# Two attentions and a recurrence ahead of the feed-forward layers: transposes, projections and norms taken in another order

## The chip, the cores and the metric

The kernel runs on one core of a Trainium2 chip. The metric is the device time of one execution in microseconds: 1994.58 as the median of three runs (1994.4 to 1996.17). Engines are TensorE (PE: products and transposes), VectorE (DVE), ScalarE (ACT), GpSimd (POOL) and SyncE (SP, which issues nearly all transfers).

## The reference

Two transformer layers are computed for 256 positions of width 1024. The change touches the first one, up to its feed-forward part. In the reference it reads, cut to that part:

```
h = rms_norm(x, attn_norm); proj = h @ w_in
lru_out = (hf + hb) * gelu(yg)            # two gated recurrences over the 256 positions, forward and back
q = rms_norm((c_q @ w_uq) per head, q_norm);  k = rms_norm(concat(k_nope, k_rope), k_norm)   # 8 heads of 96
q, k: the last 32 of 96 columns rotated (rope)
mla_out = softmax(q k^T * 96 ** -0.5) v
mixed = concat(rms_norm(lru_out), rms_norm(mla_out));  x = x + mixed @ w_out
q = rms_norm((rms_norm(x) @ w_mem_q) per head);  k = rms_norm((mem_n @ w_mem_kv) per head)   # 4 heads of 128
x = x + (softmax(q k^T * 128 ** -0.5) v) @ w_mem_o
x = x + (silu(g) * u) @ w_down            # feed-forward, not changed
```

A row norm divides a row by one number. So `rms_norm(mla_out) @ w` can be taken as `mla_out @ w` whose rows are then divided, and a query's norm can be a factor on its row of scores. A rotation does not change the sum of squares that the norm needs.

## The kernel before, in words

Weights arrive as units of 128 x 2048 numbers (1 MB) in seven buffers `raw`. ScalarE rounds a unit to the high part `wh` (`hi_to(n)` makes all units below n), VectorE subtracts it to get the low part `wl` (`lo_to(n)`); there are three pairs (`SPLIT`), so the high part of unit n waits until TensorE has released unit n-3, and the load of unit n waits for the low part of unit n-7. A product is taken in three passes (`split_product`): high by high, low by high, and, after a wait for `wl`, high by low. Activations have their own high and low parts, `hTh` and `hTl`. Units 0 to 5 are `w_in`, 6 to 9 `w_mem_kv`, 10 `w_uq`, 11 `w_ukv`, 12 to 15 `w_out`, 16 and 17 `w_mem_q`, 18 and 19 `w_mem_o`, from 20 on the feed-forward weights.

Each engine runs a list written out by hand; engines meet at semaphores (`reached(name, count)`). Nothing is planned or reordered. The order of the stages on TensorE: norm of x and `w_in`; gates of the recurrence; memory keys and values; `w_uq`, the ones-product that sums the squares of the recurrence (`lru_ssq`), `w_ukv`; transposes of query and key heads (`mla_qkT_ps`, line 536, 16 and 16); `attention("mla")`, eight heads in a pipeline of scores, transposed probabilities and weighted values, with eight pieces of the first half of `w_out` (`mixed`, n = 0 and 1) between them; transposes of the attention's output (`mla_oT_ps`); the second half of `w_out` (n = 2 and 3); x transposed; `w_mem_q`; transposes; `attention("mem")`, four heads; transposes; `w_mem_o`.

On VectorE, between the recurrence and the attention, stand `head_ms` (reduction of squares per head), the scaling of the recurrence's output (`lru_std`, `lru_scaled`), and `rotated`, which multiplies a whole of 16 heads x 96 by its inverse root and then rotates: the query first, then the key. In `attention`, VectorE takes the largest score (line 1959), ScalarE the exponentials (1322) and the copy of transposed probabilities (1330), VectorE the division by the sum (1968). ScalarE functions come in table sets: a root after an exponential shows an `ACT_TABLE_LOAD`.

The softplus series for `lru_lambda` (`sp`, 8 columns, 17 tiny operations, each waiting for the last) runs on VectorE just ahead of `lo_to(8)`.

## Time and profile before

| what | us |
|---|---|
| median of 3 runs | 1994.58 |
| profiled execution: own time / span | 1991.48 / 1989.6 |
| TensorE busy | 1883.1 (95%) |
| VectorE, ScalarE busy | 1555.6 (78%), 1253.9 (63%) |
| last chain of work, share on PE / DVE / ACT | 87% / 7% / 4% |
| first matmul on a weight unit starts | 15.33 |
| first transposes of query heads start | 111.11 |
| first scores start | 119.60 |
| memory queries' projection starts | 174.76 |
| last product of `w_mem_o` ends | 224.22 |

The part that the change touches ends at 224.22 us; the other 1765 us are the feed-forward part and the second layer. A timeline row gives start, length, engine, line, operation, output<-inputs, shapes and count, and in brackets the idle time before it with the engine that ended it. Busy time of a matmul row includes its pipeline, so the cost of one in a row of them is the distance between starts. The granted clock (PEclk) is a share of 2.4 GHz.

### The profile page before, as it was taken

What the parts mean: (1) busy time and instruction counts of PE and PEld (TensorE: products, weight loads), DVE (VectorE), ACT (ScalarE), POOL (GpSimd) and SP (SyncE); (2) the same over time, 40 slices, a digit from 0 to 9 for tenths busy, and PEclk for the clock granted to TensorE, in tenths of its full rate; (3) what the DMA queues carried; (4) which work ended last, traced back from release to release, by engine and by line L of the source; (5) the groups of instructions that cost most, each with busy time, mean ns of one, the idle gap of its engine ahead of it and who ended that gap; (6) DMA issues with size and microseconds to landing.
All of it is one profiled execution on the core that took longest, in us unless ns stands there. A gap on an engine that the chain in (4) does not pass through costs nothing.

```text
span 1989.6 us, 27408 instructions
## 1 busy us (share of the span) xinstructions
PE 1883.1 (95%) x10192; PEld 1586.2 (80%) x10192; DVE 1555.6 (78%) x1572; ACT 1253.9 (63%) x1285; POOL 11.3 (1%) x9
## 2 busy tenths in 40 slices
PE   7867899999899999998799999999999999999997
PEld 7755799887789988876688888888888888888886
DVE  7865588657656755665798998989989889899897
ACT  6854565455644435553577777777777777777775
POOL 0000000000000000000100000000000000000000
PEclk9988999999889999999899999999999999999998
DMA  8322244543225554433399998998989989999894
GB/s 356 127 101 85 85 180 181 191 171 125 85 106 189 175 188 152 149 124 105 144 370 345 339 372 322 365 364 330 367 323 361 371 326 363 330 363 367 318 367 187
DMA packets 68040, 490.83 MB, mean 247 GB/s; under 512 B 7680, under 2 KB 7936, under 8 KB 8576
## 3 DMA queue, kind: packets, MB, share of 16 engines
q1 hardware_dynamic: 67680, 488.52, 65.7%
q0 software_dynamic: 288, 1.31, 0.2%
q8 instruction: 50, 0.82, 0.2%
q14 instruction: 22, 0.18, 0.0%
HBM read 488.75 MB, written 1.05 MB: 246 GB/s over the span
## 4 chain that ended last, share of the span: by engine, by line
PE 87%; DVE 7%; ACT 4%; issue 2%; DMA 0%; SPq 0%; ACTq 0%; DVEq 0%
PE ps L399 26%; PE ps L401 20%; PE ps L408 20%; PE ps L410 5%; PE ps L403 5%; PE ps L419 2%; DVE wl L1887 1%; PE ps L1182 1%; ACT wh L1258 1%; PE ps L1094 1%; PE ps L913 1%; DVE hTl L1927 1%; PE ps L950 1%; PE ps L953 0%; PE ps L686 0%
## 5 line engine op out<-in xcount | busy, mean ns | idle before, releaser
L2713 DVE TENSOR_TENSOR wl<-raw,wh 128x2048 fp32r<-128x2048 f32 x336 | 763.1, 2289 | 81.4 <-ACT wh L1811 81.3
L1811 ACT ACTIVATE wh<-raw 128x2048 fp32r<-128x2048 f32 x336 | 642.6, 1917 | 196.3 <-PE ps L408 196.0
L399 PE MATMUL ps<-wh,work_r 128*128 128x512 f32 x1544 | 614.7, 398 | 4.0 <-DVE work_r L2718 2.4
L401 PE MATMUL ps<-wh,work_r 128*128 128x512 f32 x1544 | 613.4, 397 | 0.0
L408 PE MATMUL ps<-wl,work_r 128*128 128x512 f32 x1544 | 449.6, 396 | 0.0
L1887 DVE TENSOR_TENSOR wl<-raw,wh 128x2048 fp32r<-128x2048 f32 x125 | 286.1, 2290 | 128.0 <-ACT wh L1258 127.5
L399 PEld LDWEIGHTS ps<-wh,work_r 128*128 128x128 f32 x1544 | 290.6, 188 | 71.4 <-issue 6.9
L408 PEld LDWEIGHTS ps<-wl,work_r 128*128 128x128 f32 x1544 | 290.4, 188 | 70.2
L401 PEld LDWEIGHTS ps<-wh,work_r 128*128 128x128 f32 x1544 | 290.6, 188 | 68.9
L1258 ACT ACTIVATE wh<-raw 128x2048 fp32r<-128x2048 f32 x125 | 238.6, 1913 | 156.2 <-PE ps L408 88.9
L399 PE MATMUL ps<-hTh,wh 128*128 128x256 f32 x896 | 223.8, 287 | 2.0 <-DVE hTl L1927 1.8
L403 PE MATMUL ps<-hTl,wh 128*128 128x256 f32 x896 | 221.8, 285 | 0.0
L399 PEld LDWEIGHTS ps<-hTh,wh 128*128 128x128 f32 x896 | 173.5, 194 | 4.3 <-issue 2.6
L403 PEld LDWEIGHTS ps<-hTl,wh 128*128 128x128 f32 x896 | 173.5, 194 | 0.1
L410 PE MATMUL ps<-hTh,wl 128*128 128x256 f32 x896 | 126.3, 284 | 0.0
L410 PEld LDWEIGHTS ps<-hTh,wl 128*128 128x128 f32 x896 | 116.2, 193 | 0.0
L399 PE MATMUL ps<-wh,hTh 128*128 128x512 f32 (+1 forms) x216 | 89.3, 414 | 6.4 <-DVE hTl L2181 1.8
L401 PE MATMUL ps<-wh,hTl 128*128 128x512 f32 (+1 forms) x216 | 85.6, 397 | 0.0
L1821 ACT ACTIVATE work<-ps 128x512 f32<-128x512 f32 x56 | 33.6, 600 | 46.0 <-PE ps L408 45.9
L408 PE MATMUL ps<-wl,hTh 128*128 128x512 f32 (+1 forms) x216 | 62.6, 396 | 0.0
L419 PE MATMUL ps<-work 128*128 128x64 f32 (+2 forms) x240 | 43.5, 323 | 14.5 <-DVE xn L2293 3.4
L1496 ACT ACTIVATE xn<-ps,cols 128x256 f32<-128x256 f32 x44 | 22.4, 560 | 52.2 <-PE ps L410 52.2
(391 smaller groups left out, 1715.0 us busy)
## 6 DMA issues: line engine op xcount, KB each, us to landing
raw<-in_units SPq DMA_DIRECT2D x461, 1024.0 KB, 6.7
x<-in_x SPq DMA_DIRECT2D x1, 1024.0 KB, 4.9
work<-in_lru_w SPq DMA_DIRECT2D x1, 1024.0 KB, 15.2
xn<-in_mem SPq DMA_DIRECT2D x1, 1024.0 KB, 16.5
out<-x SPq DMA_DIRECT2D x2, 512.0 KB, 3.3
consts<-in_consts POOLq DMA_DIRECT2D x1, 768.0 KB, 4.7
work<-in_moe_gain POOLq DMA_DIRECT2D x1, 512.0 KB, 3.8
consts<-in_consts SPq DMA_DIRECT2D x1, 488.0 KB, 5.7
```

What stands on the lines that cost most here:

```text
L399: nc.tensor.matmul(out, sh, mh, start=(first and j == 0), stop=False)
L401: nc.tensor.matmul(out, sl, mh, start=False, stop=False)
L403: nc.tensor.matmul(out, sh, ml, start=False, stop=False)
L408: ins = nc.tensor.matmul(out, sh, ml, start=False, stop=done)
L410: ins = nc.tensor.matmul(out, sl, mh, start=False, stop=done)
L419: ins = nc.tensor.matmul(out, l, r, start=(first and j == 0), stop=(last and j == len(pairs) - 1))
L1258: A(wh[:, n % SPLIT, :], raw[:, n % RAW, :], ACT.Copy).then_inc(sem("hi_made"), 1)
L1496: ins = A(cv[f % 4][i], ps[:, f % 4, i * S:(i + 1) * S], ACT.Identity, scale=col("ffn_conv_w", 2 * FT + c), bias=col("ffn_conv_b", c))
L1811: A(wh[:, n % SPLIT, :], raw[:, n % RAW, :], ACT.Copy).then_inc(sem("hi_made"), 1)
L1821: A(esg, ps[:, 2 * (c % 2), :], ACT.Sigmoid).then_inc(sem("sigmoid"), 1)
L1887: V.tensor_tensor(wl[:, n % SPLIT, :], raw[:, n % RAW, :], wh[:, n % SPLIT, :].bitcast(F32), ALU.subtract).then_inc(sem("lo_made"), 1)
L2713: V.tensor_tensor(wl[:, n % SPLIT, :], raw[:, n % RAW, :], wh[:, n % SPLIT, :].bitcast(F32), ALU.subtract).then_inc(sem("lo_made"), 1)
```

## The change

- Start: `cols` is transferred first, x in two halves on two semaphores, of the constants only the first 272 of 976 columns ahead of the weights, the other 704 behind unit 2. The softplus series is taken at the very start, while x arrives, and its exponential stands ahead of the first norm.
- Recurrence to attention: the low part of unit 11 is made ahead of the backward recurrence; `w_ukv` goes ahead of the ones-product. The query is rotated without having been multiplied; its inverse root goes as a scale into the exponential (and, by one more small operation for each head, into the largest score). The key's 32 rotary columns are rotated once, before they are copied to the heads, and their squares are summed once. Buffers move so that this can overlap. VectorE's subtraction for the recurrence's output (`lru_outT`) moves behind the first largest score.
- First attention: the pieces of `w_out` start one head later. n = 0 and 1 are closed as a sum of their own and added to x during the attention (`lru_added`); the first two output chunks are transposed within head iteration 8; n = 2 and 3 are not divided by the root beforehand, but at the sum: x += r * (their product).
- Memory attention: `w_mem_q` in two units by columns (two heads each), so that two heads can be normed while the other two are projected; key transposes go ahead of the projection; the order of all steps on the three engines is written out; `w_mem_o`'s first half stands between the last two heads. The query's inverse roots are scales of the exponentials here too.

The core of the diff:

```diff
-        sp_.dma_start(x[:], x_d).then_inc(sem("x_loaded"), 16)
-        small_consts = CONST["dist"]
-        sp_.dma_start(cols[:], cols_d).then_inc(sem("params"), 16)
-        sp_.dma_start(consts[:, 0:small_consts], consts_d[:, 0:small_consts]).then_inc(sem("params"), 16)
+        sp_.dma_start(cols[:], cols_d).then_inc(sem("cols_loaded"), 16)
+        for t in range(TT):
+            sp_.dma_start(x[:, t, :], x_d[:, t, :]).then_inc(sem(f"x{t}_loaded"), 16)
+        early = CONST["reset"]
+        sp_.dma_start(consts[:, 0:early], consts_d[:, 0:early]).then_inc(sem("params"), 16)
...
+            if n == 2:
+                sp_.dma_start(consts[:, early:CONST["dist"]], consts_d[:, early:CONST["dist"]]).then_inc(sem("consts_loaded"), 16)
...
# TensorE
-        attention("mla", [lambda n=n, t=t, h=h: mixed(n, t, h, False) for n in range(2) for t in range(TT) for h in range(2)])
-        pe.wait_ge(*reached("mla_normed", TT))
-        transposes("mla_oT_ps", [mo[:, t, c * P:(c + 1) * P] for c in range(LC) for t in range(TT)], [0, 1], "")
+        def first_mixed():
+            pe.wait_ge(*reached("lru_outT", 1))
+            mixed(0, 0, 0)
+        def last_of_recurrence():
+            mixed_oT(0)
+            mixed(1, 1, 1)
+        def first_of_attention():
+            pe.wait_ge(*reached("mla_oT", 2))
+            mixed(2, 0, 0)
+        attention("mla", [lambda: None, first_mixed]
+                  + [lambda i=i: mixed(i // 4, i // 2 % 2, i % 2) for i in range(1, 7)]
+                  + [last_of_recurrence, first_of_attention])
+        mixed(2, 0, 1)
+        mixed_oT(1)
+        mixed(2, 1, 0)
+        mixed(2, 1, 1)
...
-        token_major("mem_in", UNITS_AT["w_mem_q"], hTh, hTl, (4, 5))
-        attention("mem")
-        transposes("mem_oT_ps", [eo[:, t, c * P:(c + 1) * P] for c in range(4) for t in range(TT)], [0, 1], "")
-        project_out("memory_x_change", UNITS_AT["w_mem_o"], 4, hTh, hTl, lambda k: None)
+        pe.wait_ge(*reached("mem_heads_normed", 1))
+        for u in range(2):
+            mem_turned(6 + u, [ek[:, t, h * P:(h + 1) * P] for h in (2 * u, 2 * u + 1) for t in range(TT)])
+        mem_query(0, 0)
+        mem_query(0, 1)
+        mem_query(1, 0)
+        pe.wait_ge(*reached("mem_in_copied", 5))
+        mem_turned(2, [eq[:, t, h * P:(h + 1) * P] for h in (0, 1) for t in range(TT)])
+        mem_query(1, 1)
+        mem_score(0)
+        mem_score(1)
+        pe.wait_ge(*reached("mem_in_copied", 6))
+        mem_turned(3, [eq[:, t, h * P:(h + 1) * P] for h in (2, 3) for t in range(TT)])
+        mem_turn(0)
+        mem_score(2)
+        mem_weigh(0)
+        mem_turn(1)
+        mem_score(3)
+        mem_weigh(1)
+        mem_turn(2)
+        mem_oT(0)
+        mem_weigh(2)
+        mem_turn(3)
+        mem_out(0, 0)
+        mem_out(0, 1)
+        mem_weigh(3)
+        mem_out(0, 2)
+        mem_oT(1)
+        mem_out(0, 3)
+        for q in range(4):
+            mem_out(1, q)
...
# VectorE
+        def lru_added(q):
+            dve.wait_ge(*reached("mixer_x_change", q + 2))
+            xs = x[:, q // 2, (q % 2) * HALF:(q % 2 + 1) * HALF]
+            V.tensor_tensor(xs, ps[:, 4 + q, :], xs, ALU.add).then_inc(sem("lru_added"), 1)
-        attention("mla", {1: lambda: lo_to(14), 3: lambda: lo_to(15), 4: mem_key_squares, 6: lambda: lo_to(16)})
+        attention("mla", {0: lru_low, 2: lambda: lo_to(14), 3: mem_key_squares, 4: lambda: lo_to(15),
+                          6: lambda: lru_added(0), 7: lambda: (lru_added(1), lo_to(16)),
+                          8: lambda: (lru_added(2), mla_oT_low(0), lru_added(3))})
+        mla_oT_low(1)
...
+                V.scalar_tensor_tensor(out=xs, in0=ps[:, 4 + 2 * t + h, :], scalar=osq["r"][:, t:t + 1], in1=xs,
+                                       op0=ALU.mult, op1=ALU.add).then_inc(sem("x_ready"), 1)
```

First place, VectorE from the gate product of the recurrence (`gelu`) to the first rotated heads. `wl<-raw,wh` is the low part of a weight unit, `mla_squares` the squares of the heads. Before:

```order
L2117 TENSOR_TENSOR work<-work 128x1024 [waits gelu,vector_step]
L1887 TENSOR_TENSOR wl<-raw,wh 128x2048 [waits hi_made]
L2147 TENSOR_SCALAR work<-ps 128x256 [waits lru_ssq]
L2123 TENSOR_REDUCE heads_st<-work 128x16 [waits mla_squares]
L2124 TENSOR_SCALAR heads_st<-heads_st 128x16 [waits vector_step]
L2150 RECIPROCAL work<-work 128x256 [waits std]
L2152 SCALAR_TENSOR_TENSOR work<-work,cols 128x256 [waits vector_step]
L2152 SCALAR_TENSOR_TENSOR work<-work,cols 128x256 x3
L1887 TENSOR_TENSOR wl<-raw,wh 128x2048 [waits hi_made]
L2123 TENSOR_REDUCE heads_st<-work 128x16 [waits mla_squares]
L2124 TENSOR_SCALAR heads_st<-heads_st 128x16 [waits vector_step]
L2130 RECIPROCAL heads_st<-heads_st 128x16 [waits std]
```

After (`hT_f_49`, `hT_f_50` are plain views of `hTh`, `hTl`, in which the squares and the key now lie):

```order
L2328 TENSOR_TENSOR work<-work 128x1024 [waits gelu,vector_step]
L2332 TENSOR_REDUCE heads_st<-hT_f_49 128x16 [waits mla_squares]
L2333 TENSOR_SCALAR heads_st<-heads_st 128x16 [waits vector_step]
L2340 TENSOR_TENSOR hT_f_49<-work,junk 128x256
L2341 TENSOR_TENSOR hT_f_49<-work,junk 128x256
L2342 TENSOR_TENSOR hT_f_49<-work,junk 128x256
L2343 TENSOR_TENSOR hT_f_49<-work,junk 128x256
L2344 TENSOR_TENSOR work<-hT_f_49 128x16x16 [waits vector_step]
L2345 TENSOR_TENSOR work<-hT_f_49 128x16x16
L2083 TENSOR_TENSOR wl<-raw,wh 128x2048 [waits hi_made]
L2349 TENSOR_SCALAR work<-ps 128x256 [waits lru_ssq]
```

The six query rotations stood behind two reductions, a reciprocal of 256 columns, four scalings, a weight unit and a product over 1536 columns; now they follow the first reduction. The low part of unit 11, which stood behind the gate product, stands ahead of the piece shown.

Second place, ScalarE in the memory attention, from the copy of a query projection to the third head's exponentials. `wh<-raw` is a weight unit's high part, `[waits in]` a projection, `[waits ms]` a root. Before:

```order
L1476 ACTIVATE work<-ps,small 128x512 [waits in]
L1310 ACTIVATE heads_st<-heads_st 128x8 [waits ms]
L1481 ACTIVATE work<-ps,cols 128x256 [waits qkT_ps] x8
L1322 ACT_TABLE_LOAD
L1322 ACTIVATE work,small<-ps,small 128x256 [waits att_max]
L1322 ACTIVATE work,small<-ps,small 128x256
L1322 ACTIVATE work,small<-ps,small 128x256 [waits att_max]
L1322 ACTIVATE work,small<-ps,small 128x256
L1330 ACTIVATE work<-ps 128x512 [waits att_transposed]
L1322 ACTIVATE work,small<-ps,small 128x256 [waits att_max]
```

After:

```order
L1397 ACTIVATE wh<-raw 128x2048 [waits in,raw_loaded5]
L1631 ACTIVATE work<-ps 128x2x256 [waits in]
L1645 ACTIVATE work,small<-ps,small,heads_st 128x256 [waits att_max]
L1645 ACTIVATE work,small<-ps,small,heads_st 128x256
L1625 ACTIVATE work<-ps,cols 128x512 [waits qkT_ps]
L1653 ACTIVATE work<-ps 128x512 [waits att_transposed]
L1645 ACTIVATE work,small<-ps,small,heads_st 128x256 [waits att_max]
L1645 ACTIVATE work,small<-ps,small,heads_st 128x256
L1637 ACT_TABLE_LOAD
L1637 ACTIVATE heads_st<-heads_st 128x4 [waits ms]
L1653 ACTIVATE work<-ps 128x512 [waits att_transposed]
L1645 ACT_TABLE_LOAD
```

Copies, roots, turned queries and exponentials, which followed each other as blocks, now alternate, and a root stands between the second and the third pair of exponentials, with a table load on each side.

## Rows read from the trace of the kernel before

**Rows 1.** Windows: three stretches; busy us and instructions per engine, clock, DMA, GB/s.

```profile
0.00:119.60 119.60, 86.38 (x483) 77.60 (x483) 97.67 (x173) 88.13 (x142) 0.92 (x5) 0.93 0.56 217
119.60:171.74 52.14, 45.07 (x234) 38.41 (x235) 25.81 (x45) 23.87 (x56) 0.00 (x0) 0.87 0.23 81
171.74:224.20 52.46, 40.15 (x200) 32.62 (x198) 25.36 (x38) 28.44 (x55) 0.00 (x0) 0.93 0.22 80
```

**Rows 2.** Chain of waits at the start: start us, us, what.

```profile
2.83 7.30 DMA raw<-in_units
10.16 1.92 ACT wh L1258
...
15.33 0.55 PE ps L399
...
22.45 0.96 PE ps L410 x8
```

**Rows 3.** Windows: 4 to 8 us, the input transfers.

```profile
4.00:8.00 4.00, 0.00 (x0) 0.00 (x0) 0.00 (x0) 2.26 (x5) 0.00 (x0) 1.00 1.02 400
```

**Rows 4.** Windows: the stretch of the softplus series on VectorE.

```profile
58.22:61.18 2.96, 2.96 (x15) 2.48 (x14) 2.48 (x17) 2.96 (x10) 0.00 (x0) 1.00 0.00 0
```

**Rows 5.** Timeline of TensorE, 82 to 122 us; brackets: idle before, releaser.

```profile
84.42 0.61 PE L408 MATMUL ps<-wl,consts_r 128*128 128x384 f32 x2 [1.24 <-DVE wl L1887]
...
91.73 3.65 PE L419 MATMUL ps<-work,consts 128*128 128x256 f32 x8 [3.55 <-ACT work L1424]
...
111.11 3.62 PE L536 MATMUL ps<-consts,work 128*96 128x128 f32 x16 [12.93 <-DVE work L2144]
115.23 2.13 PE L536 MATMUL ps<-consts,work 128*96 128x128 f32 x16 [0.51 <-DVE work L2144]
119.60 1.13 PE L419 MATMUL ps<-work 96*128 96x256 f32 x4 [2.23 <-ACT work L1452]
```

**Rows 6.** Timeline of VectorE, from 89 to 111 us.

```profile
89.27 1.23 DVE L2117 TENSOR_TENSOR work<-work 128x1024 f32<-128x1024 f32 x1
...
95.76 1.74 DVE L2123 TENSOR_REDUCE heads_st<-work 128x16 f32<-128x1536 f32 x1
...
106.94 1.76 DVE L2131 TENSOR_TENSOR work<-work,heads_st 128x1536 f32<-128x1536 f32 x1
...
110.54 0.42 DVE L2144 TENSOR_TENSOR work<-work 128x256 f32<-128x256 f32 x1
```

**Rows 7.** Timeline of TensorE, 145 to 230 us.

```profile
149.12 1.40 PE L419 MATMUL ps<-work 128*128 128x64 f32 x8 [0.73 <-ACT work L1330]
...
158.00 0.80 PE L399 MATMUL ps<-wh,hTh 128*128 128x512 f32 x1 [1.84 <-DVE hTl L2181]
...
174.76 0.47 PE L399 MATMUL ps<-wh,hTh 128*128 128x512 f32 x1 [1.28 <-DVE hTl L1927]
...
191.21 1.97 PE L536 MATMUL ps<-consts,work 128*128 128x128 f32 x8 [5.29 <-DVEq L2196]
```

**Rows 8.** Chain of waits, 158 to 224 us: ends of output products.

```profile
160.08 0.85 PE ps L408 x2
...
164.46 0.46 PE ps L408 x2
...
223.75 0.47 PE ps L408 x2
```

**Rows 9.** Groups by line and shape, 171.74 to 224.2 us: busy us, mean ns.

```profile
L1322 ACT ACTIVATE work<-ps,small 128x256 f32<-128x256 f32 x8 | 3.7, 470 | 2.4 <-DVE small L1959 2.4
...
L1887 DVE TENSOR_TENSOR wl<-raw,wh 128x2048 fp32r<-128x2048 f32 x4 | 9.1, 2288 | 2.5 <-ACT wh L1258 2.5
...
L1950 DVE TENSOR_TENSOR x<-ps,x 128x512 f32<-128x512 f32 x4 | 2.8, 692 | 7.4 <-PE ps L408 7.4
```

**Rows 10.** Timeline of ScalarE: a table load and what follows.

```profile
149.08 1.28 ACT L1310 ACT_TABLE_LOAD   x1
150.38 0.21 ACT L1310 ACTIVATE heads_st<-heads_st 128x8 f32<-128x8 f32 x1
```

More of the change, by code:

```diff
@@ L593, in _ @@
         release(UNITS_AT["w_uq"], "mla_q")
-        pe.wait_ge(*reached("mla_q_copied", 1))
-        pe.wait_ge(*reached("lru_sq", 1))
-        counted(accumulate(ps[:, 0, 0:S], [(ones, th[0][:, c, :]) for c in range(LC)]), "lru_ssq")
         w = unit(UNITS_AT["w_ukv"])
@@ L605, in _ @@
         release(UNITS_AT["w_ukv"], "mla_kv")
+        pe.wait_ge(*reached("mla_q_copied", 1))
+        pe.wait_ge(*reached("lru_sq", 1))
+        counted(accumulate(ps[:, 0, 0:S], [(ones, th[0][:, c, :]) for c in range(LC)]), "lru_ssq")
         pe.wait_ge(*reached("lru_ms", 1))
@@ L619, in mixed @@
                                 [(hTh[:, 2 * n + k, ts], hTl[:, 2 * n + k, ts], w[0][:, k, hs], w[1][:, k, hs])
-                                 for k in range(2)], first=(n == 0), last=last)
-            if last or h == 1 and t == 1:
+                                 for k in range(2)], first=(n % 2 == 0), last=(n % 2 == 1))
+            if n % 2 == 1 or h == 1 and t == 1:
                 counted(ins, "mixer_x_change")
@@ new lines, in _, with mem_turned, mem_query @@
+        mixed(2, 0, 1)
+        mixed_oT(1)
+        mixed(2, 1, 0)
+        mixed(2, 1, 1)
+        pe.wait_ge(*reached("mla_oT", LC))
+        for t in range(TT):
+            for h in range(2):
+                mixed(3, t, h)
+        norm("mem_attn_norm")
+        def mem_turned(bank, blocks):
+            for j, src in enumerate(blocks):
+                ins = nc.tensor.transpose(ps[:, bank, j * P:(j + 1) * P], src, ident)
+            counted(ins, "mem_qkT_ps")
+        def mem_query(u, t):
+            n = UNITS_AT["w_mem_q"] + u
+            w = by_k(unit(n), KD, S)
+            ts = slice(t * P, (t + 1) * P)
+            ins = split_product(ps[:, 4 + u, t * S:(t + 1) * S],
+                                [(hTh[:, k, ts], hTl[:, k, ts], w[0][:, k, :], w[1][:, k, :]) for k in range(KD)],
+                                ready=tile_ready)
+            if t == 1:
+                counted(ins, "mem_in")
+                release(n, "mem_in")
@@ new lines, in mem_oT, with mem_out @@
+        def mem_oT(g):
+            pe.wait_ge(*reached("mem_att_out", 2 * g + 2))
+            for c in (2 * g, 2 * g + 1):
+                for t in range(TT):
+                    ins = nc.tensor.transpose(ps[:, MEM_OT[g], (c % 2) * S + t * P:(c % 2) * S + (t + 1) * P],
+                                              eo[:, t, c * P:(c + 1) * P], ident)
+            counted(ins, "mem_oT_ps")
+        def mem_out(n, q):
+            at = UNITS_AT["w_mem_o"] + n
+            w = by_k(unit(at), 2, D)
+            t, h = q // 2, q % 2
+            ts, hs = slice(t * P, (t + 1) * P), slice(h * HALF, (h + 1) * HALF)
+            pe.wait_ge(*reached("mem_oT", n + 1))
+            ins = split_product(ps[:, 4 + q, :], [(hTh[:, 2 * n + k, ts], hTl[:, 2 * n + k, ts], w[0][:, k, hs], w[1][:, k, hs])
+                                                  for k in range(2)], first=(n == 0), last=(n == 1))
+            if n == 1 or q == 3:
+                counted(ins, "memory_x_change")
+            if q == 3:
+                release(at, "memory_x_change")
@@ L1327, in attention @@
                     act.wait_ge(*reached(stage + "_att_transposed", j + 1))
+                    if j == 0 and stage == "mla":
+                        act.wait_ge(*reached("lru_outT", 1))
                     if j >= 2:
@@ new lines, in _ @@
+        mem_turned(0)
+        mem_turned(1)
+        hi_to(UNITS_AT["w_mem_o"] + 1)
+        mem_query(0)
+        mem_query_std(0)
+        mem_turned(2)
+        A(warm, ones[:, 0:1], ACT.Exp)
+        hi_to(UNITS_AT["w_mem_o"] + 2)
+        mem_query(1)
+        mem_exponentials(0)
+        mem_turned(3)
+        mem_probsT(0)
+        mem_exponentials(1)
+        mem_query_std(1)
+        mem_probsT(1)
+        mem_exponentials(2)
+        mem_oT_high(0)
+        mem_probsT(2)
+        mem_exponentials(3)
@@ new lines, in mem_oT_low @@
+        def mem_oT_low(g):
+            dve.wait_ge(*reached("mem_oT_hi", g + 1))
+            V.tensor_tensor(hTl[:, 2 * g:2 * g + 2, :], ps[:, MEM_OT[g], :].rearrange("p (a b) -> p a b", a=2),
+                            hTh[:, 2 * g:2 * g + 2, :].bitcast(F32), ALU.subtract).then_inc(sem("mem_oT"), 1)
+        mem_query_ms(0)
+        lo_to(UNITS_AT["w_mem_o"] + 1)
+        mem_query_scale(0)
+        mem_max(0)
+        mem_query_ms(1)
+        mem_max(1)
+        mem_query_scale(1)
+        mem_weighted(0)
```

364 lines of the change are left out of this document (238 added, 126 removed).

## The prediction

> **What bounds the kernel now.** I read the page's chain first: it runs almost wholly on TensorE, so only TensorE's idle time, its granted clock and its work can move the end. The engine shares in slices then show where it is not full: the first ninth of the span. Cut in three at the first score and at the last product of the first attention's output, that part lasts 119.6, 52.1 and 52.5 us, with 86, 45 and 40 us of TensorE work and a mean granted clock of 0.93, 0.87 and 0.93 [rows 1]. Behind it TensorE has hardly a gap and nothing is changed, so what is won by 224.2 us should stay won. DMA moves 80 to 217 GB/s in these stretches [rows 1], against 400 where it is the limit [rows 3]: weights are no bound. The waits on TensorE's timeline are what the change can remove: 1.24, 3.55, 12.93 and 2.23 us up to the first attention [rows 5], 0.73 and 1.84 behind it, 5.29 in the memory attention [rows 7]. They also cost clock: six output products of 512 columns take 0.43 us each (0.85 for two, the 1.2 GHz level) just behind such a wait, and 0.23 once it has gone back to 2.4 GHz [rows 8].
>
> I follow the new order along the lists of the three engines with the durations of the rows, from landmark to landmark. Times are on the clock of the profiled span.
>
> **Start, -0.9 us.** The first product starts at 15.33. Behind it stand the first unit's landing (2.83 + 7.30), its rounding (10.16 to 12.08) and its low part [rows 2]. 704 of 976 constant columns, 0.36 MB, now follow unit 2; at 400 GB/s [rows 3] that is 0.9 us. The softplus series, 2.96 us [rows 4], now runs ahead of the norm, while x arrives; it should end at about 7, x's squares at about 7.8, so I charge nothing. If `cols` lands 2 us late, it costs up to 1 us of the 0.9. First product: 14.4.
>
> **Recurrence to w_uq, a further -1.2.** The 2.96 us leave VectorE's list in the middle of the recurrence, but ScalarE's sigmoids, tanh and exponentials run without a gap there, and bring the roots forward only by the 0.9 of the start. Unit 10's low part is then ready about when TensorE asks, and the 1.24 us wait [rows 5] goes. Now unit 11's low part (2.29 [rows 9]) also stands ahead of the backward scan; the gate product, which ended at 90.5 [rows 6], stays there: the 0.9 and the softplus time pay for it.
>
> **Query transposes from 111.11 to 97.3 us (-13.8).** This is the large term. From the gate product's end at 90.6 VectorE does: reduction 1.7 (95.76 [rows 6]), 0.2, six rotations from 108.73 on at 0.34 between starts, the last being 110.54 to 110.96 [rows 6], together 2.2, a weight unit 2.2, the 0.4 us operation on the ones-product. That ends at 97.3. The ones-product must have been computed (3.65 at the low clock [rows 5]) and its squares taken on ScalarE, about 92.4 + 3.7 = 96.1: just under. Gone from ahead of the transposes are the reciprocal of 256 columns, four scalings, one weight unit, and the product of 1536 columns, 1.76 [rows 6]. The key follows with reduction 1.2, root, reciprocal and the same 1.76: ready at 101.1. I keep 3.62 us for each 16 transposes (the low clock) although the second lot took 2.13 [rows 5]. Query 97.3 to 100.9, key 101.2 to 104.8.
>
> **First score from 119.60 to 105.8 (-13.8).** ScalarE copies the last heads after a table load that stood before the first exponential (the wait of 2.23 there [rows 5] was for such copies). What is late next is ScalarE, not VectorE: the four query copies, 1.28 of load, four key copies. At 2.4 GHz the landmark would be the same.
>
> **First attention and w_out, 52.1 us become 45.3; end 171.74 to 151.1 (-20.6).** From 150.5 (149.12 + 1.40) to 158.0 TensorE before had only transposes and waits [rows 7]; of this 7.5 us the transposes (1.8 at full clock) stay, the rest (-5.7) goes, because half of the output is turned inside iteration 8, and the root is applied at the sum. Twelve matmuls ran at 0.43 from 158.00 on (by 164.46 they were at 0.23 [rows 8]) and should run at 0.23: -2.4. The table load leaves the path ahead of the first exponential, 1.28 (of the kind in [rows 10]), and the wait of 0.73 at the last head [rows 7] has a product in it. Against this: the first piece waits for the recurrence's low part, 1.4 (VectorE takes it after the first largest score); `mixed(2, 0, 0)` waits for copy, addition to x and low part, 1.3, with the weighted values of the last head queued behind it; VectorE has an operation more for each head and the key squares between two weight units, 0.6. Together -6.8; 1.4, 1.3 and 0.6 are what the lists give, with no row of their own, so 0 to 6 for the three is the bound that goes into the range. The four additions during the attention are 0.69 each [rows 9], beside TensorE's steady 3.5 us for a head.
>
> **To the memory queries, 174.76 to 155.5 (-19.3).** The additions at the sum wait for the root (squares, table load, key heads' scaling, a weight unit: about 7.6 us after the last copy), half a us after the last product. Before, three of four were hidden behind products; now all four come behind, 4 x 0.6. The gap from product to query projection grows from 3.0 to 4.4, of which eight key transposes use 0.9. The addition now also multiplies by a column; the trace has no such form. It reads and writes what the plain one does, 0.69; between that and twice that, I take 0.69.
>
> **Memory attention, 49.5 us become 42.5; end 224.2 to 198.0 (-26.2).** Query work is 96 matmuls of 256 columns at 0.12 (eight in 0.96 [rows 2]), 11.5 us, where 48 of 512 at 0.23 made 11.0: no difference. Output products are 11.0 as before. What lay between and around was 27.5 before, the 5.29 included. Now, from the last query product on, ScalarE's list is the path: a weight unit 1.9 and the second query copy, late by 2.8; copy 0.6; three pairs of exponentials at 0.47 and 0.2 for the sum (0.9 a pair [rows 9]); probabilities copied 0.6 twice; the turned query 0.6; two table loads of 1.28, of which 1.5 is exposed and the rest lies beside VectorE; a high part, a copy, the fourth pair and a turn, 2.6; two waits for the largest score of about 1. That is 15, and 1.3 of weighted values and turns stand between the output products. The sum so far is 38.8, to 194.3. I add clock: TensorE waits 1 to 2 us at a time here, and just before the projection 4. After such waits it worked at 1.2 GHz for some us [rows 8]; 1.7 for the projection and 2.0 for attention and output: 198.0.
>
> The Trainium skill speaks against this stage. ScalarE: Activation LUTs, What ACT_TABLE_LOAD costs, says that a change of set costs the load and a drain of 1380 ns, 2.66 us together. By that the two changes here would cost another 2.8 us. The trace disagrees: the load at 149.08 takes 1.28 and the root follows at 150.38 [rows 10], with no room for a drain, so the sum keeps 1.28.
>
> **Sum.** -0.9 -1.2 -11.7 -0 -6.8 +1.3 -6.9 = -26.2 us. The profiled execution took 1991.5 (span 1989.6 and 1.9 around it), so 1965.3 by its own time. It lies 3.1 below the median of the runs, 1994.58; by the median I forecast 1968.4. Less than 0.2%, 4 us, cannot be told from no change.
>
> **Rivals.**
> - *The memory stage wins nothing* (0.22). Its 30 handoffs between three engines eat what the blocks cost before: ScalarE waits for VectorE's largest score of one head while the roots of the next stand in front. For it: my chain leaves VectorE's list untouched, and `mem_query_ms(1)` waits for ScalarE with `mem_max(1)` queued behind. Against: the block order had 5.29 us of nothing [rows 7], and a weight unit and projection now lie inside. It would be 49.5 long: -19.3, time 1975.3.
> - *The clock stays up* (0.18). No gap is long enough, and the 3.7 us of clock and 1 us at the start of the attention are not paid: -30.9, 1963.7. Against: the products just behind a wait were slow in both attentions' tails [rows 8], and before the key transposes too [rows 5].
> - *Weights are late* (0.04). The loads of the stretch come 27 us closer together. Price: the second and third stretches carried 80 GB/s in 52 us; even at 100 they are far below 400 [rows 1, 3]. If slots were released late and half of the gain were lost by it: 1981.5.
> - *Slower: the clock stays at 1.2 GHz* through the denser but still broken work from 97 to 197 us (0.03). At full clock that work is about 79 us (45 + 40 busy in the last two stretches [rows 1], less some 6 of slow clock), so at half it needs 79 more, of which some 20 fit into waits: +59 -26, time 2027. It turns the sign once about half of the stretch is so. Against it: products that began at 158.00 behind a long broken stretch were back at 0.23 by 164.46 [rows 7, 8], and the mean clock of all three stretches is 0.87 or more [rows 1].
>
> The forecast itself has 0.53, and -22 to -30 as its own range (1964.6 to 1972.6). Faster: forecast, both first rivals and most of the third, 0.95; same 0.02; slower 0.03. The range holds the first two rivals and the bound of the three unshown waits: 1960 to 1977; what lies outside is worth about 0.15.
>
> **What would show it.** In the changed kernel's trace: query transposes near 97 and first score near 106 (if the first is near 104 or later, the ones-product or ScalarE's squares hold it); no wait of more than 2 us between 106 and 151; ScalarE loads tables twice more between the exponentials of the memory heads, 1.28 each; w_mem_o ending near 198; clock under 1.0 at 97 to 105, near 155 and between 170 and 185. The feed-forward part should have the same length as before. I am wrong if the stretch from the first score to the last product of w_out stays above 48 us, or the memory stage above 47.

## The result and the profile after

The changed kernel takes 1967.72 us (median of four, 1965.09 to 1972.97), beside 1994.51 of the kernel before (1994.4 to 1996.17): ratio 0.9867, interval 0.9846 to 0.9888. Measured again with five runs it was 1968.36 (1964.6 to 1971.53). The profiled execution took 1968.23, its span is 1966.3 against 1989.6.

Windows of the changed kernel, cut at the same three places as [rows 1]: first score, end of w_out, end of w_mem_o.

```profile
0.00:106.64 106.64, 85.89 (x482) 76.92 (x483) 93.12 (x172) 85.12 (x147) 0.92 (x5) 0.94 0.63 243
106.64:150.60 43.96, 40.83 (x232) 35.07 (x232) 27.66 (x53) 26.41 (x57) 0.00 (x0) 1.00 0.20 73
150.60:196.76 46.16, 41.06 (x249) 34.45 (x248) 27.13 (x49) 30.84 (x55) 0.00 (x0) 0.96 0.28 96
```

The three stretches lasted 119.6, 52.1 and 52.5 us and now last 106.6, 44.0 and 46.2. In the second TensorE had 45 us of work at a mean clock of 0.87; it has 41 at 1.00. TensorE's timeline shows which waits are left:

```profile
83.54 0.63 PE L426 MATMUL ps<-wl,consts_r 128*128 128x384 f32 x2 [0.25 <-DVE wl L2083]
93.90 3.75 PE L437 MATMUL ps<-work,consts 128*128 128x256 f32 x8 [3.75 <-ACT work L1583]
98.41 3.65 PE L554 MATMUL ps<-consts,work 128*96 128x128 f32 x16 [0.76 <-DVE work L2349]
102.36 2.11 PE L554 MATMUL ps<-consts,hT_f 128*96 128x128 f32 x16 [0.31 <-DVE hT_f L2359]
106.64 1.99 PE L437 MATMUL ps<-work 96*128 96x256 f32 x8 [2.17 <-ACT work L1596]
110.30 0.50 PE L417 MATMUL ps<-wh,hTh 128*128 128x512 f32 x1 [1.66 <-DVE hTl L2371]
138.20 0.50 PE L417 MATMUL ps<-wh,hTh 128*128 128x512 f32 x1 [1.47 <-DVE hTl L2392]
151.45 2.63 PE L450 MATMUL ps<-consts,x 128*128 128x128 f32 x16 [0.69 <-DVE x L2414]
155.13 0.36 PE L417 MATMUL ps<-wh,hTh 128*128 128x256 f32 x1 [0.18 <-DVE hTl L2123]
170.38 0.66 PE L688 MATMUL ps<-consts,work 128*128 128x128 f32 x4 [0.51 <-ACT work L1631]
171.47 0.66 PE L718 MATMUL ps<-consts,work 128*128 128x128 f32 x4 [0.44 <-ACT work L1645]
176.53 1.13 PE L437 MATMUL ps<-xn,work 128*128 128x128 f32 x8 [0.96 <-DVE work L2448]
178.57 0.66 PE L718 MATMUL ps<-consts,work 128*128 128x128 f32 x4 [0.91 <-ACT work L1645]
180.83 1.74 PE L437 MATMUL ps<-xn,work 128*128 128x128 f32 x8 [1.18 <-ACT work L1653]
```

Of [rows 5] the 12.93 us ahead of the query transposes have become 0.76; of [rows 7] the 5.29 in the memory attention are gone, and five waits of 0.4 to 1.2 stand there instead.

Stages of all profiles, from their timelines. A: start of the first product on a weight unit. B: first product of w_uq with a low part to the first score. C: first score to the memory projection. D: projection to the end of w_mem_o. E: the rest, which is the same code everywhere. A is a point in time, the others are lengths; the stretch between A and B, 66.6 to 69.9 us, is not listed.

| kernel | A | B | C | D | E | span |
|---|---|---|---|---|---|---|
| before | 15.33 | 35.18 | 55.16 | 49.45 | 1765.4 | 1989.6 |
| before, again | 15.47 | 35.16 | 55.14 | 49.47 | 1768.4 | 1992.7 |
| changed | 15.76 | 23.10 | 48.49 | 41.63 | 1769.5 | 1966.3 |
| changed, again | 16.48 | 23.06 | 48.48 | 40.16 | 1767.2 | 1962.8 |
| mem_block | 16.22 | 22.92 | 48.52 | 51.46 | 1765.6 | 1971.3 |
| one_table | 15.99 | 23.09 | 48.51 | 42.55 | 1768.4 | 1966.4 |
| norm_first | 16.07 | 22.89 | 55.37 | 40.16 | 1770.2 | 1971.8 |
| x_whole | 15.04 | 23.11 | 52.11 | 40.15 | 1768.4 | 1965.4 |
| start_back | 16.13 | 23.10 | 48.49 | 40.17 | 1768.1 | 1962.8 |
| turned_late | 15.63 | 22.82 | 48.06 | 41.61 | 1770.3 | 1966.0 |
| mult_back | 15.19 | 24.89 | 48.15 | 42.59 | 1770.4 | 1968.6 |
| softplus_late | 15.52 | 23.41 | 50.44 | 40.16 | 1767.0 | 1966.4 |
| rotated_late | 16.62 | 30.23 | 50.32 | 41.63 | 1769.6 | 1974.9 |
| combined | 14.49 | 21.05 | 48.98 | 41.59 | 1766.4 | 1959.2 |

Where the edit lies in the start or in a later stage, B repeats within 0.3 us and C, but for x_whole, within 0.1. A does not repeat: with x in halves it lies anywhere from 15.19 to 16.62. D, with the order of the change, comes at 40.16 (five times), 41.6 (four times) or 42.6 (once).

Seven rows come from runs of a single execution, of which nothing but the stages can be compared: x_whole 1967.22 us, start_back 1964.62, turned_late 1967.79, mult_back 1970.38, softplus_late 1968.17, rotated_late 1976.67, before, again 1994.57.

### The profile page after: what moved, and what is told of

The parts are those of the page before. It is cut to its first block, busy times and chain, and to the rows that moved or that the text cites. A ratio compares the mean times of both kernels' runs of the same rounds, so it can differ in the third digit from the quotient of the medians.

```text
span 1966.3 us, 27547 instructions
## 1 busy us (share of the span) xinstructions
PE 1883.0 (96%) x10240; PEld 1586.1 (81%) x10240; DVE 1554.5 (79%) x1589; ACT 1255.5 (64%) x1290; POOL 11.3 (1%) x9
## 4 chain that ended last, share of the span: by engine, by line
PE 87%; DVE 6%; ACT 5%; issue 1%; DMA 0%; SPq 0%; ACTq 0%; DVEq 0%
PE ps L417 26%; PE ps L419 20%; PE ps L426 20%; PE ps L421 6%; PE ps L428 6%; DVE wl L2083 2%; PE ps L437 1%; PE ps L1318 1%; ACT wh L1397 1%; PE ps L1230 1%; PE ps L1049 1%; PE ps L822 1%; PE ps L823 1%; PE ps L827 1%; PE ps L1086 1%
## 5 line engine op out<-in xcount | busy, mean ns | idle before, releaser
L417 PE MATMUL ps<-wh,hTh 128*128 128x512 f32 (+2 forms) x232 | 90.4, 394 | 5.2 <-DVE hTl L2371 1.7
L419 PE MATMUL ps<-wh,hTl 128*128 128x512 f32 (+2 forms) x232 | 86.3, 376 | 0.0
L426 PE MATMUL ps<-wl,hTh 128*128 128x512 f32 (+2 forms) x232 | 61.3, 373 | 0.0
L417 PEld LDWEIGHTS ps<-wh,hTh 128*128 128x128 f32 x232 | 44.2, 191 | 14.8 <-issue 3.5
```

The lines of the kernel that those rows point to most:

```text
L417: nc.tensor.matmul(out, sh, mh, start=(first and j == 0), stop=False)
L419: nc.tensor.matmul(out, sl, mh, start=False, stop=False)
L426: ins = nc.tensor.matmul(out, sh, ml, start=False, stop=done)
```

## The experiments

**again, before_again: where 4 us went.** By w_mem_o's end the change was ahead by 27.5 us (224.2 against 196.8), at the end of the span by 23.3.

> The changed kernel unchanged, a second time. Its profiled execution stood 27.6 us ahead of the kernel before at the last product of w_mem_o (196.6 against 224.2 us) and only 23.3 us ahead at the end: 4.3 us were given back in stages that the change does not touch. Theory A (the granted clock of sparse unchanged stages falls differently from one execution to the next): the landmarks up to 196.6 repeat within 0.3 us, the rest, 1769.7 us, comes out different by 1 to 5 us, and the place of the difference has another granted clock. Theory B (something that the change does systematically, such as the place at which weights arrive): the rest is again 1769 to 1770.5 us, with slow clock in the same places.

> The kernel before, profiled a second time. Its unchanged rest behind the last product of w_mem_o took 1765.4 us in the first profile; in nine profiles of changed kernels it was 1765.6 to 1770.6. Theory A (chance of the granted clock in sparse stretches): the rest lies in the same band, 1764 to 1776, and the stretches at the low clock lie elsewhere than in the first profile. Theory B (the change makes the rest longer by 2 to 4 us): the rest is again below 1766.

The changed kernel's rest was 1767.2 the second time, that of the kernel before 1768.4, 3.0 more than the first time: theory A holds; the twelve changed profiles lie at 1765.6 to 1770.4. Two readings in again miss their expectation, that the landmarks repeat within 0.3 us: the first product came 0.7 later, and D differed by 1.5. The 3.0 us between the two profiles of the kernel before arise from 823 to 943 us. Windows of unchanged code, first profile, then second:

```profile
820.00:840.00 20.00, 20.00 (x166) 18.46 (x165) 11.73 (x22) 10.28 (x17) 0.00 (x0) 1.00 0.62 211
...
860.00:880.00 20.00, 20.00 (x114) 15.86 (x112) 17.52 (x15) 15.09 (x18) 0.00 (x0) 1.00 0.35 127
```

```profile
820.00:840.00 20.00, 20.00 (x155) 18.59 (x156) 11.29 (x20) 8.89 (x15) 0.00 (x0) 0.91 0.51 192
...
860.00:880.00 20.00, 20.00 (x100) 15.98 (x99) 17.49 (x16) 14.49 (x17) 0.00 (x0) 0.92 0.36 128
```

TensorE has no gap in these windows either time, and yet begins 155 matmuls for 166 and 100 for 114, at a clock of 0.91 and 0.92 for 1.00. Eleven timed runs of the kernel before in one comparison agree: the fastest took 1989.99 us at a mean clock of 0.974, the slowest 2001.71 at 0.968. The first profile of before had a short rest. Whether the change itself costs one or two us of the rest is open: two profiles of before are too few.

**mem_block: is it the order that wins in the memory stage?**

```diff
-  key turns, mem_query(0, 0) ... mem_weigh, mem_out: all alternating
+  token_major("mem_in", ...); norms; transposes; attention("mem"); transposes; project_out(...)
```

> The changed kernel with the memory stage in the order of before: w_mem_q by its halves, all heads projected, then normed, turned, attended, output turned, w_mem_o, each as a block. Theory A (the gain of the stage, 49.5 to 41.5 us, is its order): the stage is 49 to 50 us, the last product of w_mem_o ends near 204.6, the time rises by 8 us to some 1975.5. Rival B (half of the gain or more is the granted clock that stayed up, since TensorE comes warm out of a denser first attention): the stage is 45 or less, w_mem_o ends at 200 or earlier, the time rises by 4 or less.

Stage D took 51.46 us, 9.8 to 11.3 more than with the new order; the time went to 1973.87 (ratio 0.9891, 0.987 to 0.9912) beside 1968.36 in the same comparison. The rows, in the block order:

```profile
170.67 1.97 PE L554 MATMUL ps<-consts,work 128*128 128x128 f32 x8 [5.29 <-DVEq L2288]
175.27 3.78 PE L437 MATMUL ps<-work 128*128 128x256 f32 x8 [0.93 <-ACT work L1542]
```

The wait of 5.29 is back to the hundredth [rows 7]. Theory A, the order, holds (49 to 50 expected); the stage is even 2.0 longer than in the kernel before, where the eight scores took 1.99, not 3.78: the low clock fell on them. The median rose by 5.5 where 8 were expected, and in the profiled execution E was short, 1765.6; the stage, not the total, is the evidence.

**one_table: are the two table loads worth removing?**

```diff
+        mem_query(1)
+        mem_turned(3)
+        mem_query_std(1)
         A(warm, ones[:, 0:1], ACT.Exp)
-        hi_to(UNITS_AT["w_mem_o"] + 2)
-        mem_query(1)
         mem_exponentials(0)
-        mem_turned(3)
         mem_probsT(0)
         mem_exponentials(1)
-        mem_query_std(1)
         mem_probsT(1)
         mem_exponentials(2)
+        hi_to(UNITS_AT["w_mem_o"] + 2)
```

The edit does more than move a root: the high part of a weight unit, 1.9 us of ScalarE, goes from ahead of the first exponential to behind the third pair, and VectorE squares the second two heads ahead of the first largest score.

> Both inverse roots of the memory queries ahead of the first exponential, so that the two table loads of 1.28 us between the memory exponentials (at 174.0 and 176.0) go. Theory A (ScalarE's list is the path of the stage): the third pair of exponentials starts near 174 in place of 177.3, w_mem_o ends near 193.5, 3 us earlier, the time falls by 3 to some 1964.5. Rival B (the root needs the last projection's squares and so only stands in front of the first exponentials, which then start 1.6 us or more later, and VectorE's largest scores hold the rest): w_mem_o ends at 196 to 197, no change.

Timeline of ScalarE, of the changed kernel, then of one_table:

```profile
170.22 0.56 ACT L1645 ACTIVATE work<-ps,small,heads_st 128x256 f32<-128x256 f32 x1
...
174.01 1.28 ACT L1637 ACT_TABLE_LOAD   x1
175.31 0.21 ACT L1637 ACTIVATE heads_st<-heads_st 128x4 f32<-128x4 f32 x1
...
176.02 1.28 ACT L1645 ACT_TABLE_LOAD   x1
177.31 0.56 ACT L1645 ACTIVATE work<-ps,small,heads_st 128x256 f32<-128x256 f32 x1
...
180.66 0.57 ACT L1645 ACTIVATE work<-ps,small,heads_st 128x256 f32<-128x256 f32 x1
```

```profile
171.43 1.28 ACT L1669 ACT_TABLE_LOAD   x1
...
172.83 0.55 ACT L1645 ACTIVATE work<-ps,small,heads_st 128x256 f32<-128x256 f32 x1
...
179.50 0.56 ACT L1645 ACTIVATE work<-ps,small,heads_st 128x256 f32<-128x256 f32 x1 [0.29 <-DVE small L2440]
...
183.35 0.58 ACT L1645 ACTIVATE work<-ps,small,heads_st 128x256 f32<-128x256 f32 x1
```

The first exponential starts 2.6 us later (172.83 for 170.22), although the high part no longer stands ahead of it, TensorE waits 3.48 for it, and the third pair starts at 179.50, not 174. Theory A falls. The fourth pair starts 27.9 us behind the projection where it was 25.5. Whether the stage as a whole loses is less sure: D is 42.55, that is 0.9 or 2.4 more than in the two profiles of the changed kernel, but mult_back, with the order of the change, has 42.59, and the low clock lies elsewhere in each. The time was 1972.27 (ratio 0.9878, 0.9854 to 0.9902) beside 1968.36, and the two intervals overlap. So nothing is won, which is what rival B expected, though w_mem_o ends at 198.0 and not at 196 to 197; the loads are the price of starting two heads before the other two are normed.

**norm_first and turned_late: what shortened the first attention's tail?**

```diff
 both:            attention("mla", ... + [last_of_recurrence])     # mixed_oT(0) and mixed(2, 0, 0) behind it
 norm_first only: V.tensor_scalar(mo[:, t, :], mo[:, t, :], osq["r"][:, t:t + 1], None, ALU.mult)   # ahead of the transposes
                  V.tensor_tensor(xs, ps[:, 4 + 2 * t + h, :], xs, ALU.add)                         # plain sum
```

> The first attention's output is multiplied by its inverse root ahead of the transposes, as before the change, and added to x plainly; no output chunk is turned inside head iteration 8, and n = 2 and 3 of w_out come after the attention. The root's chain (squares, table load, root) then stands between the last head and the transposes. Theory A, the step of the prediction (7.5 us of transposes and waits shrink by 5.7, and 2.4 us of slow clock behind them go): w_out ends 8 to 11 us later than in the changed kernel (150.6), at 159 to 162, and the time rises by about as much less the 3 us that the root costs at the sum, to 1974 to 1977. Rival B (turning inside the iteration and the norm at the sum win little; the gain of the stretch is the low part, the piece order and the table load): w_out ends below 155, the time rises by 3 or less.

> No output chunk turned inside head iteration 8 and all of n = 2 and 3 of w_out behind the attention; the norm stays at the sum. With the output also normed ahead of the transposes the stretch from the first score to the end of w_out had been 52.2 us against 44.0. Theory A (the root's chain ahead of the transposes is what costs; turning early is small): stretch 45 to 46, w_out ends 1 to 2 us later than in the changed kernel. Rival B (turning inside the iteration is what takes away the 5.7 us, as the prediction has it): 49.5 or more.

Rows of TensorE, first from norm_first, then from turned_late: the output's transposes, the first product behind them, x's transposes, the memory projection.

```profile
142.77 1.97 PE L654 MATMUL ps<-consts,work 128*128 128x128 f32 x8 [5.27 <-DVE work L2407]
145.73 0.79 PE L417 MATMUL ps<-wh,hTh 128*128 128x512 f32 x1 [0.99 <-DVE hTl L2395]
158.24 1.91 PE L450 MATMUL ps<-consts,x 128*128 128x128 f32 x16
161.43 0.36 PE L417 MATMUL ps<-wh,hTh 128*128 128x256 f32 x1 [0.40 <-DVE hTl L2126]
```

```profile
137.34 1.27 PE L654 MATMUL ps<-consts,work 128*128 128x128 f32 x8
139.91 0.50 PE L417 MATMUL ps<-wh,hTh 128*128 128x512 f32 x1 [1.29 <-DVE hTl L2394]
150.93 1.91 PE L450 MATMUL ps<-consts,x 128*128 128x128 f32 x16
154.11 0.36 PE L417 MATMUL ps<-wh,hTh 128*128 128x256 f32 x1 [0.40 <-DVE hTl L2125]
```

From first score to the end of w_out: 44.0 us changed, 52.2 norm_first (158.24 - 106.06; 52.0 before), 44.9 turned_late (150.93 - 106.05). The root's chain ahead of the transposes costs 7.3 of the 8.2, its wait of 5.27 and slow matmuls behind it; turning early is worth 0.9, and by the projection it has cost 0.4 (C 48.06 for 48.49). In turned_late x's transposes start without a wait and take 1.91 us. In the changed kernel they wait 0.69 for VectorE's first addition and then take 2.63, in four groups of four, each of which starts 0.66 behind the last, as the additions come; the granted clock is 1.00 in both. norm_first's time rose by 4.0 only, to 1972.35 (ratio 0.9876, 0.9853 to 0.9899), though C is 6.9 longer. Of theory A the stretch holds (8.2 longer, 8 to 11 expected), the time, 1974 to 1977, does not.

**mult_back, softplus_late, rotated_late: what made the first score 13 us earlier?**

```diff
 mult_back:     + step(V.tensor_tensor(mq[:], mq[:], ones..., ALU.mult))        # ahead of the six rotations
 softplus_late: the 17 operations of sp back behind gelu_z, in the recurrence
 rotated_late:  the six rotations and mk *= root behind lru_scaled
```

> One more product over 16 x 96 columns on VectorE (with ones) ahead of the query's six rotations, where the norm's factor was applied before. Theory A (VectorE is the path from the gate product to the query transposes, the ones-product just under it): query transposes and first score 1.8 us later, 100.2 and 108.4 where the start is that of the changed kernel's profile. Rival B (ScalarE's squares and the ones-product, whose end at 97.65 left only 0.76 us, hold the landmark): 0.2 to 1.0 us later. In either case the transposes wait for VectorE for 2.0 to 3.3 us in place of 0.76.

> The 17 operations of the softplus series back in the middle of the recurrence on VectorE, the rest as in the changed kernel. In eight executions in which the series stands at the start the stretch from the first product of w_uq to the first transposes of the query took 14.87 us, whatever the clock did. Theory A, the prediction's (ScalarE's sigmoids, tanh and exponentials are the path of the recurrence, and the series was hidden in it but for a rest): the low part of unit 10 comes later by no more than 1 us, and the first score 0.9 later. Rival B (VectorE is the path there): everything from the first product on a weight unit to the first score is longer by the full 2.96 us.

> The six rotations of the query and the key's product with its root moved behind the reciprocal of 256 columns and the four scalings of the recurrence's output, where they stood before. Theory A (order on VectorE makes the landmark: reciprocal 1.74, scalings 1.7, then 2.2 of rotations and 1.76 for the key in a row): query transposes 7.5 us later, first score 6.5 to 7.5 later (30 us behind the first product of w_uq in place of 23.1), of which the first piece of w_out gives back its own wait of 1.66. Rival B (ScalarE's copies and roots hold the first score): 4 or less.

TensorE, mult_back, softplus_late and rotated_late in turn:

```profile
92.97 2.58 PE L437 MATMUL ps<-work,consts 128*128 128x256 f32 x8 [3.75 <-ACT work L1583]
99.27 3.65 PE L554 MATMUL ps<-consts,work 128*96 128x128 f32 x16 [3.73 <-DVE work L2350]
```

```profile
85.37 0.88 PE L426 MATMUL ps<-wl,consts_r 128*128 128x384 f32 x2 [1.24 <-DVE wl L2083]
96.63 3.75 PE L437 MATMUL ps<-work,consts 128*128 128x256 f32 x8 [3.15 <-ACT work L1583]
100.90 2.77 PE L554 MATMUL ps<-consts,work 128*96 128x128 f32 x16 [0.52 <-DVE work L2349]
```

```profile
105.19 3.62 PE L554 MATMUL ps<-consts,work 128*96 128x128 f32 x16 [8.40 <-DVE work L2363]
```

In mult_back one product of 1536 columns costs its full 1.79 (B 24.89 for 23.10): VectorE is the path, theory A. Rotating late costs 7.1 (30.23), theory A; C then grows by 1.8 where 1.66 were expected back: scores and first pieces ran at a clock of 0.50. In softplus_late rival B is nearer. The loss lies ahead of B: from the first product on a unit to w_uq's low part 69.9 us for 67.8, with the wait of 1.24 back to the hundredth [rows 5]. VectorE reaches the reduction of the query's squares at 93.56 for 91.73, though the memory keys' products, up to which nothing differs, started 0.2 earlier (71.24 for 71.45): 2.0. The first score is 2.1 later (108.78 for 106.64), by that mark 2.4 of the 2.96. The row that could have told is in the trace of the kernel before: from 55.83 us to the gate product's end VectorE, third in the row, is busy for 33.74 of 34.58 us and waits for nobody, ScalarE for 30.35.

```profile
55.83:90.41 34.58, 30.92 (x142) 25.67 (x142) 33.74 (x55) 30.35 (x53) 0.00 (x0) 1.00 0.35 125
```

With the series gone, VectorE waits once in that stretch for ScalarE, 0.48 us; so both are near the path, VectorE first. Behind its first score softplus_late was at a low clock too, and C was 50.44.

**x_whole, start_back: why did the first product come later?**

```diff
-        for t in range(TT):
-            sp_.dma_start(x[:, t, :], x_d[:, t, :]).then_inc(sem(f"x{t}_loaded"), 16)
+        sp_.dma_start(x[:], x_d).then_inc(sem("x0_loaded"), 16)
```

> x in one transfer, cols still ahead of it, 704 constant columns still behind unit 2. In five executions of the changed start (this kernel, and four others that share it) the first unit's transfer was issued at 3.08 us and took 7.50 to 8.21, against 2.83 and 7.30 in the kernel before. Theory A (the halves of x, with rows of 4 KB in place of 8 KB, slow the queue): issue at 2.62, transfer 7.1 or less, the first product on a weight unit near 14.9. Rival B (it is the short rows of the 272 constant columns, or cols ahead of x): only the 0.46 us of one issue go, the transfer stays 7.5 to 8.2 and the first product starts at 15.3 to 16.0.

> All transfers ahead of the first unit as in the kernel before (x whole, then cols, then all 976 constant columns at once); the rest of the change stays. Theory A (the new order of the transfers costs the 0.4 us or more by which the first product came late): issue of the first unit at 2.83, transfer 7.3, first product 15.3. Rival B (the start varies by as much from one execution to the next, whatever the order): anywhere from 15.3 to 16.5. The softplus series then waits for cols behind x and should run from about 5 to 8.5 us, ahead of the norm; the second half's statistics start up to 1 us later.

With x in halves the first unit is issued at 3.08 and its transfer took 6.92 to 8.36 us in nine profiles, A 15.19 to 16.62; with x whole, here and in `combined`, issue 2.61, transfer 7.25 and 6.69, A 15.04 and 14.49, both below all nine. So one issue of 0.46 is certain. That the transfer itself gets shorter is not shown: 7.25 occurs with halves too (softplus_late), and x_whole hit neither theory's range (7.1 or less, 7.5 or more). In start_back the unit was issued at 2.91 and landed at 10.52, for 10.57 in the changed kernel and 10.13 in the one before, and A is 16.13, but from another cause: the softplus operations wait for `cols` behind x and push the norm, whose transposes start only at 12.78. With the old order of transfers softplus first is bad; `cols` first belongs to it.

x_whole won 2.0 us at the first score (104.69 for 106.64), 0.7 of them at the first product and 1.2 while the first unit was worked off (32 matmuls begin in 16 to 20 us, 21 in the changed kernel). It had lost them by the projection (156.80 for 155.13). Windows of x_whole, then of the changed kernel:

```profile
108.00:112.00 4.00, 3.18 (x8) 2.11 (x8) 1.91 (x3) 3.73 (x9) 0.00 (x0) 0.50 0.01 2
112.00:116.00 4.00, 4.00 (x15) 3.37 (x14) 0.93 (x3) 0.95 (x2) 0.00 (x0) 0.62 0.00 0
```

```profile
108.00:112.00 4.00, 2.34 (x11) 1.61 (x11) 2.65 (x5) 3.27 (x6) 0.00 (x0) 1.00 0.01 2
112.00:116.00 4.00, 4.00 (x28) 3.61 (x27) 1.35 (x5) 2.56 (x10) 0.00 (x0) 1.00 0.00 0
```

The work is the same and starts 2 us earlier; the clock is at 0.50 and 0.62 (1.2 GHz for all or most of the time), and C is 3.6 longer. It is tempting to blame the earlier start, but other profiles speak against it: softplus_late and rotated_late start later (108.78 and 113.40), were at the low clock there too, and have C of 50.44 and 50.32; combined starts earliest of all (102.22) and was not. Which of them it strikes is open.

```profile
112.00:116.00 4.00, 3.24 (x9) 2.55 (x10) 1.47 (x3) 3.30 (x7) 0.00 (x0) 0.50 0.00 2
```

That is softplus_late, 3.2 to 7.2 us behind its first score.

**combined.**

```diff
 x_whole and turned_late, and:
-        lo_to(13)                                     # VectorE, behind the query's rotations
+        lo_to(13)                                     # behind lru_scaled
-  ones-product in ps[:, 0], its operation ahead of the key's reduction
+  ones-product in ps[:, 7], its operation behind the key's reduction
```

> What the runs so far point to, together: x in one transfer; no output chunk turned inside head iteration 8; and between recurrence and attention the ones-product in bank 7, so that the query transposes no longer wait for the operation on it, with the low part of unit 12 behind the scalings of the recurrence instead of ahead of the key's reduction. By the rows of the changed kernel: first product 0.5 to 0.9 earlier; key ready 2.1 earlier, first score 1.5 to 2 earlier (21.3 us behind the first product of w_uq in place of 23.1); memory projection a further 0.4 earlier. Theory A (these are the path, and the clock falls alike): -2.8 in all, 1965.5 median. Rival B (a stretch that starts earlier falls into another pattern of the clock, as with x in one transfer, where 2 us won at the first score were lost by the end of w_out): 1967 to 1970, no change.

```profile
94.81 2.12 PE L554 MATMUL ps<-consts,work 128*96 128x128 f32 x16
98.87 1.95 PE L554 MATMUL ps<-consts,hT_f 128*96 128x128 f32 x16 [1.95 <-DVE hT_f L2360]
102.22 1.99 PE L437 MATMUL ps<-work 96*128 96x256 f32 x8 [1.40 <-ACT work L1598]
106.78 0.50 PE L417 MATMUL ps<-wh,hTh 128*128 128x512 f32 x1 [2.56 <-DVE hTl L2373]
```

B is 21.05 (21.3 expected), 2.05 less; the first piece of w_out gives 0.9 of it back (2.56 for 1.66). In its profile w_mem_o ends at 192.8, 2.8 to 4.0 ahead of the two profiles of the changed kernel, and the span is the shortest of all. The times do not show it: 1966.39 (1960.97 to 1970.2, four runs) is inside the spread of the changed kernel, and the ratio to before, 0.9866 (0.9849 to 0.9883), is the same as its 0.9867; theory A had 1965.5, rival B 1967 or more, and 1966.39 decides neither. It is a better order in the trace and no faster kernel that these runs can prove.

## Why the prediction was right, and where it was not

The forecast by the median was 1968.4, the result 1967.72. The steps:

- **Start, -0.9: wrong, +0.4 and +1.1 in the two profiles of the changed kernel (-0.1 to +1.3 in all nine with this start).** The forecast took the constants that moved behind unit 2 as time won. The transfer did not get shorter (7.50 for 7.30), and the second issue of x came in front of it; the window that answers to [rows 3] has 319 GB/s, not 400:

```profile
4.00:8.00 4.00, 0.00 (x0) 0.00 (x0) 2.57 (x15) 2.94 (x6) 0.00 (x0) 1.00 0.95 319
```

  Of the added instructions I had not counted the second issue. Why the rate is lower was not separated further from the short rows of the 272 columns that stayed in front.
- **w_uq, -1.2: the wait went (1.24 to 0.25), for another reason.** I had ScalarE as the recurrence's path and softplus as hidden; softplus_late shows VectorE as the path, and 2.0 to 2.4 us of softplus on it. The sum held because I let the low part of unit 11 (2.29) be paid by it.
- **Query transposes at 97.3, first score at 105.8: 98.41 and 106.64.** Late by 1.1 and 0.8. The gate product ended at 91.8 where 90.6 was taken, which is nearly the 1.4 that the start missed. That a late start is carried on so is true of this profile, not in general: mem_block starts 0.5 later and has its transposes 0.8 earlier (97.66). VectorE's list, item by item, was right: mult_back puts the 1.76 at 1.79, rotated_late the order at 7.1.
- **First attention and w_out, 45.3 us: 44.0.** The two new waits were put at 1.4 and 1.3, and are 1.66 and 1.47. The clock stayed at 1.00 throughout. The reason given for the -5.7 was half wrong: turning inside iteration 8 brings 0.9 us by w_out's end and nothing by the projection; the norm at the sum brings 7.3 with the clock behind it.
- **To the projection, 155.5: 155.13.** The addition that multiplies by a column takes 0.74 each (2.7 us for four) where 0.69 to 1.38 was the bound.
- **Memory attention, 42.5 us: 41.6, and 40.2 in five other profiles.** The chain of 38.8 was 1.4 short of the 40.2: handoffs of 0.4 to 1.2 us stand between all engines. (The terms listed for its 15 us add up to 14.0.) The 3.7 us of clock were too much; 0 to 2.4 were paid, from 22 to 32 us behind the start of the projection, never at the projection itself. The two errors cancel, which is luck. The loads cost 1.28 each: behind the one at 174.01 the root starts at 175.31. The Trainium skill (ScalarE: Activation LUTs, What ACT_TABLE_LOAD costs) adds a drain of 1380 ns to each; no run here shows one.
- **"What is won by 224.2 us should stay won": not in this pair of profiles.** 27.5 us were won and 23.3 arrived. The forecast of the profiled execution, 1965.3, was therefore 2.9 too low, although w_mem_o ended 1.2 earlier than forecast. Adding 3.1 for the median of before made the final number right, partly by luck: it stood for just such a rest.

Of the rivals, "the clock stays up" was true of the first attention and half true of the memory stage; "the memory stage wins nothing" falls by mem_block. No wait of TensorE from 106 to 197 us is for a transfer, so "weights are late" falls, and the mean clocks of 1.00 and 0.96 there rule out the slower one.

## What to carry to other kernels

A norm that divides rows belongs at the sum behind the product: its chain of squares, table load and root was 7.3 of the 8.2 us gained in one stretch, the finer interleaving beside it less than one. Where engines alternate by heads, a table load in the middle can be no dearer than holding all heads back for one root. Judge such edits by the length of their own stage in the trace: the same code differs by 3 us between profiles and by 12 between runs, with the mean clock between 0.974 and 0.968, so that a real gain of 1 to 3 us in a stage does not show in the total.

## What the runs showed of the hardware

- An unchanged stretch can cost 1.8 to 3.6 us more from one kernel to the next: the first 10 us of the first attention ran at a granted clock of 1.00 in the changed kernel and of 0.5 to 0.6 in x_whole, which started 2 us earlier, and fell to 0.50 in softplus_late and rotated_late, which started 2 and 7 us later.
- The memory stage takes 40.16, 41.6 or 42.6 us and hardly anything between, and its first 12 output products of 512 columns took 3.0 us in the first case (again) and 3.6 to 3.9 in the others (combined, mult_back): whole stretches at a lower level, no drift.
- An exponential of 256 columns whose scale is a computed column takes 0.56 us; with a constant scale it took 0.47 [rows 9]. The 16 of the first attention stay hidden: TensorE waits for no exponential there. What the 8 of the memory attention cost was not measured; TensorE waits 0.44 and 0.91 us for two of their pairs.
- Moving 0.36 MB from ahead of the first 1 MB transfer to behind it did not bring its landing forward while x came in two halves (10.57 us for 10.13 in the changed kernel); with x whole it landed at 9.85 and 9.30 (x_whole, combined).
